# Output and embedding products in three rounded passes, with weights rounded between attention units

## The reference

```python
for i in range(2):
    proj = h @ w_in[i] + b_in[i]                       # 1024 -> 2560
    conv_out = conformer_conv(...)                     # 512 channels
    attn_out = neighbourhood_attention(q, k, v, rpb)   # 8 heads of 64
    mix = concatenate([conv_out, attn_out]) @ w_out[i] + b_out[i]
    h = layer_norm(ALPHA * h + mix, ln1_g[i], ln1_b[i])
    f = swiglu(h) if i == 0 else moe_swiglu(h)
    e = sigmoid(h @ ple_gate_w[i] + ple_gate_b[i]) * (p[i] @ ple_w[i])
    h = layer_norm(ALPHA * h + f + e, ln2_g[i], ln2_b[i])
```

## Time and profile before

| | |
|---|---|
| median of 3 runs | 2195.8 us (2193.78 to 2198.14) |
| the profiled execution | 2192.72 us, span 2191.0 us, mean granted clock 0.994 |
| busy, share of the span | TensorE 98%, VectorE 70%, ScalarE 58%, GpSimd 6% |
| attention units, layer 0 | 622.3 to 646.7 us of the span |
| output and embedding products, layer 0 | 646.7 to 681.2 us |
| the same in layer 1 | 1008.3 to 1042.8 us |
| mixture of experts | from about 1077 us to 2175 us |

### The profile page before, as it was taken

The page is one execution under the profiler, slowest core; times in us unless marked ns, Lnnn a source line. Parts: engine busy times, 40 slices in busy tenths (PEclk is TensorE's granted clock), DMA queues, the critical chain, the costliest instruction groups (busy, mean ns, idle before and its releaser), DMA issues.

```text
span 2191.0 us, 30457 instructions
## 1 busy us (share of the span) xinstructions
PE 2139.8 (98%) x11381; PEld 1745.1 (80%) x11381; DVE 1541.9 (70%) x1331; ACT 1262.6 (58%) x1263; POOL 139.3 (6%) x149
## 2 busy tenths in 40 slices
PE   9999999998999999999899999999999999999997
PEld 8977797886866999875677888888888888888875
DVE  5756543456435655625798888888888888888887
ACT  6755443333343433324567777776777767777673
POOL 0032020000200300010030000000000000000100
PEclk9999999999999999999999999999999999999999
DMA  5522494212835555372599999999999999999995
GB/s 212 195 84 97 173 356 153 97 58 103 252 134 189 195 190 189 138 216 93 177 351 404 371 370 384 369 377 370 368 376 367 379 365 383 366 377 370 379 397 192
DMA packets 85459, 581.50 MB, mean 265 GB/s; under 512 B 9969, under 2 KB 9969, under 8 KB 19457
## 3 DMA queue, kind: packets, MB, share of 16 engines
q1 hardware_dynamic: 75728, 544.77, 65.9%
q0 software_dynamic: 9184, 34.54, 4.4%
q10 hardware_dynamic: 464, 1.02, 0.1%
HBM read 559.91 MB, written 15.73 MB: 263 GB/s over the span
## 4 chain that ended last, share of the span: by engine, by line
PE 85%; DVE 7%; DMA 3%; issue 2%; ACT 2%; POOL 1%; POOLq 0%; DVEq 0%; ACTq 0%; SPq 0%
PE bank L577 75%; DVE wrest L2384 3%; DMA arena<-arena 2%; PE bank L1289 1%; DMA ring<-in_w_moe 1%; POOL arena L501 1%; PE bank L781 1%; PE bank L913 1%; PE bank L808 1%; DVE h L2135 1%; PE bank L1097 1%; PE bank L911 1%; PE bank L1115 1%; PE bank L890 0%; PE bank L892 0%
## 5 line engine op out<-in xcount | busy, mean ns | idle before, releaser
L2384 DVE TENSOR_TENSOR wrest<-ring,whi 128x2048 fp32r<-128x2048 f32 x378 | 852.9, 2303 | 92.1 <-ACT whi L1744 90.4
L1744 ACT ACTIVATE whi<-ring 128x2048 fp32r<-128x2048 f32 x374 | 697.0, 1917 | 80.2 <-DMA ring<-in_w_moe 78.2
L577 PE MATMUL bank<-whi,xgT 128*128 128x512 f32 x1008 | 404.9, 402 | 4.8 <-DVE wrest L2384 3.5
L577 PE MATMUL bank<-wrest,xgT 128*128 128x512 f32 x1008 | 396.7, 394 | 0.0
L577 PE MATMUL bank<-whi,xgR 128*128 128x512 f32 x1008 | 393.7, 391 | 0.0
L577 PEld LDWEIGHTS bank<-whi,xgT 128*128 128x128 f32 x1008 | 189.6, 188 | 50.4 <-DVE wrest L2384 8.6
L577 PEld LDWEIGHTS bank<-whi,xgR 128*128 128x128 f32 x1008 | 189.5, 188 | 46.3
L577 PEld LDWEIGHTS bank<-wrest,xgT 128*128 128x128 f32 x1008 | 188.9, 187 | 38.7
L577 PE MATMUL bank<-whi,hidE 128*128 128x512 f32 x504 | 201.7, 400 | 4.0 <-DVE hidR L2389 3.9
L577 PE MATMUL bank<-wrest,hidE 128*128 128x512 f32 x504 | 198.2, 393 | 0.0
L577 PE MATMUL bank<-whi,hidR 128*128 128x512 f32 x504 | 196.7, 390 | 0.0
(11 more groups left out here) (426 smaller groups left out, 3728.5 us busy)
## 6 DMA issues: line engine op xcount, KB each, us to landing
ring<-in_w_moe SPq DMA_DIRECT2D x378, 1024.0 KB, 4.8
ring<-in_w_dense SPq DMA_DIRECT2D x135, 1024.0 KB, 4.8
row<-in_rows POOLq DMA_DIRECT2D x17, 512.0 KB, 7.5
xg_rows<-ncT POOLq DMA_DIRECT2D x12, 512.0 KB, 19.8
y_rows<-arena POOLq DMA_DIRECT2D x9, 512.0 KB, 6.5
arena<-xg_rows SPq DMA_DIRECT2D x9, 512.0 KB, 5.3
arena<-arena POOLq DMA_DIRECT2D x32, 142.0 KB, 7.6
arena<-in_tbias POOLq DMA_DIRECT2D x2, 1536.0 KB, 16.4
```

What stands on the lines that cost most here:

```text
L577: ins = pe.matmul(out_, lhsT, rhs, start=start, stop=stop, **more)
L1744: S["w_hi"].on(a.activation(whi[:, n % HI_SLOTS, :], ring[:, c % RING, :], ACT.Copy))
L2384: S["w_lo"].on(v.tensor_tensor(wrest[:, s, :], ring[:, s, :], whi[:, n % HI_SLOTS, :].bitcast(F32), ALU.subtract))
```

## The change

The output product and the embedding product are also made in three passes, in both layers. What moves where:

- ScalarE rounds chunks 0 to 2 of the output product in quarters of 512 columns, one in each of the units 3 to 14; VectorE takes the rests of chunks 0 and 1 in quarters in units 7 to 14. Chunks 3 and 4 are rounded, and the rests of 2 to 4 taken, beside the output product.
- The attention result, the convolution result and the embedding input get rounded and rest parts (`catH`, `catR`, `pTH`, `pTR`).
- Gate chunks 0 and 1 are rounded once the third output chunk is used, and VectorE takes their rests ahead of the layer norm. Gate chunk 2 is rounded after the embedding result is copied, and its rest taken after the norm (in layer 1 after the router's top-2).
- `weigh2` now issues through `mm`, so that the twelfth chunk of the layer is given back during attention. A semaphore on VectorE's last additions of the feed-forward result is replaced by the engine's own step semaphore, and its second wait is dropped.

The core of the diff, cut ("..." marks what is left out):

```diff
-PROJ_CHUNKS, GATE_CHUNKS = 10, 4
-LAYER_CHUNKS, CONV_AT, GATE_AT = 21, 8, 17
+PROJ_CHUNKS, MIX_CHUNKS, GATE_CHUNKS = 10, 5, 4
+LAYER_CHUNKS, CONV_AT, MIX_AT, GATE_AT = 21, 8, 12, 17
+MIX_EARLY = 3
...
+        catH = (rounded("catH0", 5248, 4, SEQ), rounded("catH1", 6272, 4, SEQ))
+        catR = (rounded("catR0", 8320, 4, SEQ), rounded("catR1", 4096, 4, SEQ))
+        pTH, pTR = rounded("pTH", 10816, 2, SEQ), rounded("pTR", 11328, 2, SEQ)
+        mhi = (rounded("mhi0", 0, CHUNK)[:, :], phi[2], phi[0], rounded("mhi3", 0, CHUNK)[:, :], phi[2])
...
-                        ins = pe.matmul(ps[4 + j][:, c], p2T[:, u % 2, b * P:(b + 1) * P], v2[:, b, c],
-                                        start=b == 0, stop=b == 1, skip_group_check=True)
+                        ins = mm(ps[4 + j][:, c], p2T[:, u % 2, b * P:(b + 1) * P], v2[:, b, c],
+                                 start=b == 0, stop=b == 1, skip_group_check=True)
...
                     if k == 0:
-                        wait(pe, "aT_done", 2 * (i + 1))
+                        wait(pe, "cat_lo", 3 * i + 2)
                         wait(pe, "cn_done", 3 * (i + 1))
                     if k == 4:
-                        wait(pe, "cat_done", 4 * (i + 1))
-
-                rows_out(catT, KT, 4, S["mix_ps"], before_mix)
-
-                pe.wait_ge(pT_in, 16 * (i + 1))
-                rows_out(pTs, 2, 4, S["pp_ps"], None, lambda q: wait(pe, "mix_done", 4 * i + q + 1))
+                        wait(pe, "cat_lo", 3 * i + 3)
+
+                def split_mix(m):
+                    wait(pe, "w_lo", RESTS[i] + PROJ_CHUNKS + m + 1)
+                    return split_chunk(m, mhi[m], 2)
+
+                for m in range(3):
+                    wh, wr = split_mix(m)
+                    for k in (2 * m, 2 * m + 1):
+                        before_mix(k)
+                        for q in range(4):
+                            j, n = divmod(q, 2)
+                            x = (slice(None), k % 4, slice(j * P, (j + 1) * P))
+                            col = slice(n * 512, (n + 1) * 512)
+                            split_product(ps[4 + q][:, :], (catH[k // 4][x], catR[k // 4][x]),
+                                          (wh[:, k % 2, col], wr[:, k % 2, col]), k == 0, False)
+                    give(1)
+                wh, wr = split_mix(3)
+                for j in range(2):
+                    for k in (6, 7):
+                        x = (slice(None), k % 4, slice(j * P, (j + 1) * P))
+                        for n in range(2):
+                            col = slice(n * 512, (n + 1) * 512)
+                            ins = split_product(ps[4 + 2 * j + n][:, :], (catH[1][x], catR[1][x]),
+                                                (wh[:, k % 2, col], wr[:, k % 2, col]), False, k == 7)
+                    S["mix_ps"].on(ins)
+                give(1)
+                wh, wr = split_mix(4)
+                for j in range(2):
+                    for k in range(2):
+                        x = (slice(None), k, slice(j * P, (j + 1) * P))
+                        for n in range(2):
+                            if k == 0:
+                                wait(pe, "mix_done", 4 * i + 2 * j + n + 1)
+                            col = slice(n * 512, (n + 1) * 512)
+                            ins = split_product(ps[4 + 2 * j + n][:, :], (pTH[x], pTR[x]),
+                                                (wh[:, k, col], wr[:, k, col]), k == 0, k == 1)
+                    S["pp_ps"].on(ins)
+                give(1)
...
+                    if 3 <= u < 15:
+                        m, part = divmod(u - 3, 4)
+                        c = LAYER_FIRST[i] + MIX_AT + m
+                        if part == 0:
+                            a.wait_ge(ready[c % RING], 16 * (c // RING + 1))
+                            a.wait_ge(chunks_used.sem, LAYER_FIRST[i] + MIX_AT)
+                        x = slice(part * 512, (part + 1) * 512)
+                        ins = a.activation(mhi[m][:, x], ring[:, c % RING, x], ACT.Copy)
+                        if part == 3:
+                            S["w_hi"].on(ins)
...
-                    S["aT_done"].on(a.activation(catT[:, 0:4, j * P:(j + 1) * P],
+                    S["aT_done"].on(a.activation(catH[0][:, :, j * P:(j + 1) * P],
...
                 for f in range(4):
-                    S["cat_done"].on(a.activation(catT[:, 4 + f, :], cc[:, f, :], ACT.Silu,
...
-                for m in range(3):
-
-                    round_dense(LAYER_FIRST[i] + GATE_AT + m, phi[m % 3], 3, LAYER_FIRST[i] + CONV_AT + 4)
+                a.wait_ge(S["cat_done"].sem, S["cat_done"].n)
+                S["cat_done"].on(a.activation(catH[1][:, :, :], csq[:, :, :], ACT.Copy))
+                a.wait_ge(pT_in, 16 * (i + 1))
+                S["cat_done"].on(a.activation(pTH[:, :, :], pTs[:, :, :], ACT.Copy))
+                for m, used in ((MIX_AT + 3, MIX_AT + 1), (MIX_AT + 4, MIX_AT + 2)):
+                    round_dense(LAYER_FIRST[i] + m, mhi[m - MIX_AT], 3, LAYER_FIRST[i] + used)
+                for m in range(2):
+                    round_dense(LAYER_FIRST[i] + GATE_AT + m, phi[m % 3], 3, LAYER_FIRST[i] + MIX_AT + 3)
                 for q in range(4):
                     j, n = divmod(q, 2)
                     wait(a, "pp_ps", 2 * i + j + 1)
                     S["ple_act"].on(a.activation(ppx[:, j, n * 512:(n + 1) * 512], ps[4 + q][:, :], ACT.Copy))
+                round_dense(LAYER_FIRST[i] + GATE_AT + 2, phi[2], 3, LAYER_FIRST[i] + MIX_AT + 4)
                 copy_h(2 * i + 1)
                 round_dense(LAYER_FIRST[i] + GATE_AT + 3, phi[0], 3)
...
-                if i:
-
-                    wait(v, "f_added", 4)
...
+                    if 7 <= u < 15:
+                        m, part = divmod(u - 7, 4)
+                        c = (LAYER_FIRST[i] + MIX_AT + m) % RING
+                        x = slice(part * 512, (part + 1) * 512)
+                        if part == 0:
+                            wait(v, "w_hi", ROUNDED[i] + PROJ_CHUNKS + 4 + m + 1)
+                        ins = v.tensor_tensor(wrest[:, c, x], ring[:, c, x], mhi[m][:, x].bitcast(F32), ALU.subtract)
+                        if part == 3:
+                            S["w_lo"].on(ins)
...
+                for j in range(2):
+                    x = (slice(None), slice(None), slice(j * P, (j + 1) * P))
+                    wait(v, "aT_done", 2 * i + j + 1)
+                    S["cat_lo"].on(v.tensor_tensor(catR[0][x], ps[2 + j][:, :].rearrange("p (f n) -> p f n", f=4),
+                                                   catH[0][x].bitcast(F32), ALU.subtract))
...
-                for m in range(3):
-                    rest_dense(LAYER_FIRST[i] + GATE_AT + m, phi[m % 3], gate_rounded(i, m))
+                wait(v, "cat_done", 6 * i + 5)
+                S["cat_lo"].on(v.tensor_tensor(catR[1][:, :, :], csq[:, :, :], catH[1][:, :, :].bitcast(F32), ALU.subtract))
+                wait(v, "cat_done", 6 * i + 6)
+                v.tensor_tensor(pTR[:, :, :], pTs[:, :, :], pTH[:, :, :].bitcast(F32), ALU.subtract)
+                for m in range(2, MIX_CHUNKS):
+                    rest_mix(m)
+                for m in range(2):
+                    rest_gate(m)
...
-                    rest_dense(LAYER_FIRST[i] + GATE_AT + 3, phi[0], gate_rounded(i, 3))
+                    rest_gate(2)
+                    rest_gate(3)
...
-                S["f_added"].on(v.tensor_tensor(fe[:, j, c], fe[:, j, c], ps[4 + 2 * j + n][:, :], ALU.add))
-                v.wait_ge(S["f_added"].sem, 2 * j + n + 1)
+                fin(v.tensor_tensor(fe[:, j, c], fe[:, j, c], ps[4 + 2 * j + n][:, :], ALU.add))
...
-            rest_dense(LAYER_FIRST[1] + GATE_AT + 3, phi[0], gate_rounded(1, 3))
+            for m in (2, 3):
+                rest_dense(LAYER_FIRST[1] + GATE_AT + m, phi[m % 3], gate_rounded(1, m))
```

More of the change, by code:

```diff
@@ L231, in build @@
         up, stk, sg = at(4096, 4, UP_W), at(5248, 16, STACK_W), at(8768, 4, SEQ)
-        catT, csq = at(5248, KT, SEQ), at(7296, 4, SEQ)
+        csq = at(7296, 4, SEQ)
         cc, rdiag = at(9792, 4, SEQ), at(25088, 2, P)
@@ L664, in split_rows @@
                     give(1)
-            def rows_out(src, n_k, first_bank, done, wait_k=None, free=None):
-                for k in range(n_k):
-                    if k % 2 == 0:
-                        w = chunk().rearrange("p (k n) -> p k n", k=2)
-                    if wait_k:
-                        wait_k(k)
-                    if k == n_k - 2:
-                        break
-                    for j in range(2):
-                        for n in range(2):
-                            mm(ps[first_bank + 2 * j + n][:, :], src[:, k, j * P:(j + 1) * P],
-                               w[:, k % 2, n * 512:(n + 1) * 512], start=k == 0, stop=False)
-                    if k % 2:
-                        give(1)
-                for j in range(2):
-                    for kk in (k, k + 1):
```

(9 more changed lines are left out.)

25 lines of the change are left out of this document (16 added, 9 removed).

## The result

The changed kernel takes **2209.8 us**, the median of 5 runs (2208.56 to 2215.45); the kernel before took 2195.8 beside it (2191.99 to 2199.4, 5 runs). The ratio is 1.0069, 95% interval 1.0050 to 1.0089: slower by 0.7%. The forecast was 2206.0 in a range of 2200 to 2212, so direction and range held, and 3.8 us are missing. The profiled executions are 2208.56 us (span 2206.9) and 2192.72 (span 2191.0), their spans 15.9 us apart; the medians are 14.0 apart. Executions of one kernel differ by their mean granted clock: the five of the changed kernel have 0.989, 0.988, 0.986, 0.985 and 0.981, in the order of their times from 2208.56 to 2215.45 us, and the profile shows the shortest of them.

What follows compares the result with a forecast made beforehand. TensorE time and stalls were taken as the bound. Per layer 3.7 + 0.7 - 1.0 + 1.7 = 5.1 us, two layers 10.2, on 2192.72 gives 2202.9; with 3.1 from profile to median, 2206.0 us, range 2200 to 2212.

Steps and rivals of the forecast that it cites:

- TensorE's price: Output and embedding products: each falls from 0.864 to 0.693 us; 32 of 40 count, 5.5 us less a layer.
- The quarters, +3.7: Attention units: quarter roundings on ScalarE and quarter rests on VectorE add 3.7 us a layer, ends 2.9 and 5.6.
- The subtraction, +0.7: Start of the output product: TensorE also waits for a VectorE subtraction behind ScalarE's copy, 0.7 us a layer.
- The held norm: Norm's additions wait behind two gate rests until T + 23.6 (T: output product's start); only 1.0 of 5.5 us arrives.
- The clock, +1.7 a layer: Around TensorE's 3.5 us wait for the norm: one fall of the granted clock a layer, costing 1.7 us.
- the clock stays low longer, or falls twice a layer: Rival on the granted clock in both layers: 3.4 us more than forecast, 2209.4 us; chance 0.09.
- the change doesn't do what it says: Rival: output product's three passes cost the old 0.864 us, nothing of the 5.5 us arrives, about 2217 us; chance 0.02.

Runs made afterwards that it cites:

- e8: e7 with the fillers (unneeded matmuls) of e6 around the norm; 2180.2 us, ratio 0.9950 to the kernel before.
- e1: Changed kernel without ScalarE's quarters in the units (output chunks 0 and 1 rounded whole before them), VectorE's quarters kept; ratio 1.0057 to the kernel before.
- e2: Changed kernel without any quarters: output chunks 0 and 1 rounded and their rests taken whole before the units; ratio 1.0020 to the kernel before.
- e7: e5 with the first output chunk's 16 passes on the rounded input first, the 8 with its rest after; ratio 0.9973 to the kernel before.
- e3: Changed kernel with gate chunks 0 and 1 rounded into places of their own, chunk 0 taken before output chunk 4, chunk 1 after; ratio 1.0025.
- e10: Changed kernel with unneeded filler matmuls only from the embedding product on, around the norm; ratio 1.0032 to the kernel before.
- e5: e2 and e3 together: no quarters, and own places for gate chunks 0 and 1; ratio 1.0009 to the kernel before.
- e9: Changed kernel with only the first output chunk's passes reordered, the 16 on the rounded input first; ratio 1.0066 to the kernel before.
- e4: Changed kernel with unneeded filler matmuls in four places a layer, from ahead of the output product to ahead of the gate product; ratio 1.0038.
- e6: e5 with fillers only ahead of the turned tokens' second half (2) and the gate product (1); ratio 0.9976 to the kernel before.

## Why the prediction was right, and where it was short

**TensorE's price: right.** In e8, where nothing holds them and the clock stays up, the norm's first addition comes 19.78 us after the first pass; the forecast for that case was T + 19.6 by 0.693 us a product. The Trainium skill's count of four passes (FP8 and Floating Point Precision, TensorE Precision Notes), of which three would be 0.648 us, would give 28 x 0.045 = 1.3 us less than that, an estimate. The trace does not agree with the estimate: 0.231 us a pass, 0.80 of the full product.

**The quarters, +3.7: right, and in both halves.** The terms as written add up to 3.8 (4.8 - 1.89 + 0.9), and the upper end to 5.7; the slip of 0.1 a layer is of no weight. Measured 3.73, of it 2.85 for VectorE (forecast 2.9) and 0.88 for ScalarE's side (forecast: 0.9 of waiting). e1 and e2 show it as cause. **The subtraction, +0.7: right**, 0.71 in e2, hidden in e7.

**The held norm: right.** The additions were forecast at T + 23.6 and came at T + 23.57 in layer 1. The output product brought 0.84 us there instead of 5.5, plus 0.26 in the norm itself (forecast 1.0 in all). e3 shows the two gate rests as the cause; it moves both their buffer and their order, and does not tell these apart.

**The clock, +1.7 a layer: the step that failed.** It took one fall a layer, behind the norm wait, at the price of the earlier trace rows. First, that fall was there in both layers but cost more: in layer 0 0.71 (transposes and their signal) + 2.23 (gate passes) = 2.9 us, in layer 1 1.69 + 0.72 = 2.4. It also lasted longer than the one that gave the price: the clock stood low from 686 to 695 and from 1058 to 1063, in the earlier trace rows only from 220 to 223. e10 gets these 5.4 us back. The fall around this wait stands in all 14 layers without fillers there (after, e1, e2, e3, e5, e7, e9) and in none of the 8 with them (e4, e6, e8, e10). Second, there is another fall in each layer that I did not expect: at the head of the output product in layer 0, 1.56 us, and in the tail of the units in layer 1, where VectorE sets the pace and it cost nothing (28.11 us in both layers). Together 6.9 us in the two layers where 3.4 were forecast. Without the clock the layers come to +6.7, forecast 6.8. The balance of the two profiled executions, in us:

| part | forecast | measured |
|---|---|---|
| quarters and subtraction, two layers | 8.8 | 8.9 |
| norm path, two layers | -2.0 | -2.2 |
| clock in the two layers | 3.4 | 6.9 |
| start, up to layer 0 | 0 | -1.0 |
| feed-forward stretch | 0 | 1.3 |
| expert stretch | 0 | 2.0 |
| sum | 10.2 | 15.9 |

The last three are in no forecast of mine. The first of them is not the clock's, though the kernel before had a fall in its first 30 us that the changed one lacks. Ahead of the convolution TensorE waits in both kernels for a copy by DMA, and that landed 1.0 us earlier (kernel before, then changed):

```profile
595.43 4.95 PE L577 MATMUL bank<-arena,ring 128*32 128x256 f32 x87 [2.13 <-DMA arena<-arena]
```

```profile
594.45 5.82 PE L584 MATMUL bank<-arena,ring 128*32 128x256 f32 x104 [3.42 <-DMA arena<-arena]
```

The profile of e10 has the same falls as the kernel before up to there, and starts this row at 594.50 as well. Why the copy lands earlier no run tells. The other two are falls of the clock: the changed kernel had one behind the feed-forward norm (near 906) and one at the start of the experts (near 1108). They come at the same two spots in other kernels too, each in the profiles of eight of the eleven kernels with the change, and in neither the kernel before nor e8. From layer 1's gate product (the addition behind it) to the end of the span are 1112.5 to 1114.5 us in the eight with the fall at the experts and 1110.6 to 1111.3 in the four without. The same idle time can go either way; behind the feed-forward norm it is 2.05 us in the kernel before, where the clock stayed up, and in the changed one, where it fell:

```profile
899.55 1.09 PE L984 MATMUL bank<-cst,h 128*128 128x128 f32 x8 [2.05 <-DVE h L2135]
```

```profile
906.43 1.51 PE L966 MATMUL bank<-cst,h 128*128 128x128 f32 x8 [2.05 <-DVE h L2166]
```

How often the change brings them can't be told from one profile a kernel. The rival "the clock stays low longer, or falls twice a layer" gave 2209.4 and is what happened, both halves of it; I had given it 0.09. The two layers came to 13.6 us, which is that rival's sum. That the medians differ by nearly as much, 14.0, is partly luck: outside the layers the profiles differ by another 2.3 us that no term stood for, and the profile of the kernel before lies 3.1 us below its median, that of the changed kernel 1.3. The sentence that idle gaps of 1.02 and 1.57 us cost nothing in the earlier trace rows led me there: I looked only for single long gaps.

**Left open: the first fall.** Ahead of the output product of layer 0 stand no long gaps: 1.10, 0.81, 0.46 twice and 0.41 us in the tail of the units, 1.46 before the first pass. In layer 1 the clock fell at 1013, right behind the 1.10 and the 0.81. With VectorE's quarters in the units (after, e1, e3, e4, e9, e10) the clock fell in that tail or at the output product in every layer. Without them it fell in layer 0 of e2, e5, e6 and e7, in layer 1 of e6 alone, and in neither of e8. So it is more frequent with quarters (12 of 12 layers against 5 of 10), and they are not its only condition. Without them the gaps in the tail are 0.22, 0.21, 0.25 and 0.41 us (e5); whether a filler directly ahead helps is not shown, as in e4 the clock had fallen before it, and that e7's order of passes does is not shown, as e7 and e8 have the same code up to there and differ in layer 0. A filler between the last units was not tried. Nor were raw output chunks with no rest at all.

The Trainium skill's statement that throttled is the default and activity releases it (TensorE: Matmul & The Clock Gate, "What's actually happening") agrees with what the fillers did around the norm: matmuls whose results nobody reads kept 1.00 there.

Of the rivals, the last one ("the change doesn't do what it says") is mispriced. By the prediction's own hold, passes at the old price would start the norm 24 x 0.171 = 4.1 us a layer later, which gives 2214.2 and not 2217. The passes at 0.231 us rule it out either way.

## What to carry to other kernels

Price work put between pipelined units by the free time of the engine that gets it (1.89 us was free, 4.8 us came), and look for idle time of the same engine further ahead: the same rests cost nothing before the units. When passes become cheaper, read what now stands in the program order of the engine that consumes them; here two rests waited for the buffer of the third output chunk, ahead of the norm, and ate 3.8 us a layer. And a new wait of TensorE like those of 2.73 and 3.53 us here is to be priced with the clock behind it, or filled with matmuls that nobody reads. Last, compare kernels by many executions: one profile shows where the clock fell once.

## What the runs showed that I had not expected

- The clock falls without one long gap: in the changed kernel it stood at 0.50 at 652.00 to 653.00 behind idle times of 1.10, 0.81, 0.46, 0.46, 0.41 and 1.46 us. A pass of 512 columns then takes 0.43 us from start to start instead of 0.23.
- The fall around one wait of 3.53 us cost 2.9 us in layer 0, nearly as much as the wait itself: transposes, the copies that wait for them and the first gate passes all lie behind it. Two fillers within the wait (four records, 1.88 us) and one ahead of the gate product kept the clock up there in e6 and e8.
- Executions of one kernel lie up to 16.6 us apart (e7), more than the kernel before and the changed one, and the longer ones have the lower mean granted clock.
